# Softmax division moved from the exponents into the matmul that turns them, in two of three attention branches

## The chip, the cores and the metric

The kernel runs on one core of one Trainium2 chip. Its time is the device time of one execution in microseconds (us). Three runs of the kernel before gave 1705.82, 1708.54 and 1713.55 us; the median, 1708.54 us, is what a changed kernel is held against. Five engines work side by side, each through its own list of instructions in order, and wait for each other by semaphores: TensorE (PE, matmuls; PEld is its loading of the stationary operand), VectorE (DVE), ScalarE (ACT), GpSimd (POOL) and SyncE (SP, which issues most DMAs).

## The reference

One decoder layer on a sequence of 1024 positions, width 1024, in float32. Three attention branches read one combined projection of the normalised input:

- A: three head groups of four heads with strided windows, merged by their softmax denominators;
- B, the shared-key branch: eight query heads in two groups that share a key head each, window of 128, with a learned sink in each head's denominator;
- M, the memory branch: four heads of 128 against 256 memory tokens.

Then come gates, three output projections, one common output projection, and a feed-forward block. For B and M the part that matters here is

```python
lse = jax.nn.logsumexp(s, axis=-1)
if sink is not None:
    lse = jnp.logaddexp(lse, sink...)
p = jnp.exp(s - lse[..., None])
o = jnp.einsum('nhgbqk,nhbkd->nhgbqd', p, vw)      # B
p = jax.nn.softmax(sc, axis=-1)                    # M
o = jnp.einsum('bhsm,bmhd->bshd', p, mv)
```

In words: each row of exponents (one query, up to 256 keys) is divided by the row's sum, and the quotients weigh the values.

## The kernel before

The first part of the program, `input_projections`, handles 44 jobs (`JOBS`), each the projection of one tile of 128 positions for one branch. PE walks the jobs in order; a job of branch A or B has eight slices of 3 matmuls with 512 columns and eight of 3 matmuls with 256 columns (`project`), a job of M has only the 512-column ones. Everything else of the attention hangs between these slices at fixed places. The attention of a tile is cut into pairs (`PAIRS`): one pair per tile in A and M, two per tile in B, which makes 16 pairs in B and 8 in M. A pair holds four heads as two units `u` of two heads `e`. Pairs run two jobs behind their projection (`LAG`).

For pair n, four engines work in turn:

1. PE `score(n)` writes the four heads' scores to two PSUM banks (L1336 for B, L1332 for M).
2. DVE `minima(n)` finds each row's minimum of the negated scores and for B writes them, masked, to the tile `prob` (L1049; L1038 for M).
3. ACT `exps(n)` writes the exponents to `prob`, 128 queries in the partitions by up to 256 keys, and their sums to `small` (L832); for B it also takes the exponent of the sink (L838).
4. DVE `divide(n)`: for B it adds the sink (L1069), then takes the reciprocal of four sums (L1071) and multiplies the four heads' exponents in place (L1076). After each unit it raises `prob_done`.
5. PE `turn_probs(n, u)` turns the blocks of 128x128 of unit u by a transposition against `ident` into the PSUM bank `prob_turn` (L1350); that is four blocks, or two in the first tile of B, which has no tile before it. It raises `prob_turned`.
6. ACT `copy_probs(n, u)` copies them to SBUF (`prob_t`, L845).
7. PE `weigh_values(n)` multiplies by the values (L1373), and DVE `copy_out(n)` takes the result from PSUM (L1087).

The order in PE's list is written out by hand (`step_slices`, `second_turns`, `parts`). At the step of pair n stand `turn_probs(n - 1, 0)`, `score(n)`, `weigh_values(n - 2)` in a row; `turn_probs(n - 1, 1)`, called the second turn below, stands two slices later. In DVE's list `minima(n)`, `copy_out(n - 2)`, often `normalise` of the next tile's queries and keys (L998, L1005), and two or three slices on `divide(n)` (`DIVIDE_BEHIND`). Branch A isn't divided there; its sums are used later by `merge_factors`.

`rope_cos` and `rope_sin` are tables of 3 orders of the sequence; orders 1 and 2 serve the strided groups of A, order 0 serves A's first group and B. `prob` has room for two pairs.

Of the kernel before, what the change touches and what calls it, by code (L numbers as in the profile page):

```python
# [11 lines left out]
ALU = mybir.AluOpType  # L12
# [3 lines left out]
P = 128  # L16
# [20 lines left out]
KIND = [STAGES[s][0] for s, _ in JOBS]  # L37
# [88 lines left out]
def has_prev(j):  # L126

    s, t = JOBS[j]
    kind, order = STAGES[s][:2]
    if kind == "M":  # L130
        return True
    return t > 0 if order == 0 else (t % 2 == 1 if order == 1 else False)
# [215 lines left out]
def input_projections(nc, x_t, mem_t, positions, attn_norm, w_in, a_q_norm, a_k_norm, b_q_norm, b_k_norm,  # L348
# [8 lines left out]
    with ExitStack() as ctx:  # L357
# [14 lines left out]
        rope_cos = sb("rope_cos", [P, 3, 8, ROT])  # L372
        rope_sin = sb("rope_sin", [P, 3, 8, ROT])
# [6 lines left out]
        with ExitStack() as dilated:  # L380
# [13 lines left out]
        small = sb("small", [P, 2, 20])  # L394
# [26 lines left out]
        scored, min_done, exp_done, prob_done, prob_turned, prob_copied, pv_done, o_done, sink_gap, sink_exp = (  # L421
            sem(n) for n in ("scored", "min_done", "exp_done", "prob_done", "prob_turned", "prob_copied",
                             "pv_done", "o_done", "sink_gap", "sink_exp"))
# [21 lines left out]
        prob_turn = ps[:, PT, :].rearrange("p (e b n) -> p e b n", e=2, b=2)  # L445
# [93 lines left out]
        def prob_of(n, u):  # L539
            return prob[:, 2 * (n % 2) + u, :, :]  # L540

        def unit_stats(n, u, e):

            j, v = PAIRS[n]
            s, t = JOBS[j]
            i = 2 * u + e
            if KIND[j] == "A":
                return stats[:, STAGES[s][2], t, i:i + 1], stats[:, STAGES[s][2], t, 4 + i:5 + i]
            return small[:, n % 2, i:i + 1], small[:, n % 2, 4 + i:5 + i]
# [357 lines left out]
        def _(dve):  # L907
# [154 lines left out]
            def divide(n):  # L1062
                j, v = PAIRS[n]
                kind = KIND[j]
                dve.wait_ge(exp_done, 2 * n + 2)
                total = small[:, n % 2, 4:8]
                if kind == "B":
                    dve.wait_ge(sink_exp, count_b(n) + 1)
                    link(dve.tensor_tensor(small[:, n % 2, 12:16], total, small[:, n % 2, 8:12], ALU.add))  # L1069
                    total = small[:, n % 2, 12:16]  # L1070
                link(dve.reciprocal(small[:, n % 2, 16:20], total))  # L1071
                c0 = 0 if has_prev(j) else P
                for u in range(2):
                    for e in range(2):
                        i = 16 + 2 * u + e
                        ins = dve.tensor_scalar(prob_of(n, u)[:, e, c0:256], prob_of(n, u)[:, e, c0:256],  # L1076
                                                small[:, n % 2, i:i + 1], None, ALU.mult)
                        if e == 0:
                            link(ins)
                    ins.then_inc(prob_done, 1)  # L1080
# [77 lines left out]
            for j in range(NJ + LAG + 1):  # L1158
# [24 lines left out]
                for k in range(8):  # L1183
                    if k in step_slices(j):
                        n = steps_before(j) + step_slices(j).index(k)
# [31 lines left out]
        def _(pe):  # L1217
# [122 lines left out]
            def turn_probs(n, u):  # L1340
                j = PAIRS[n][0]
                if KIND[j] == "A":
                    pe.wait_ge(exp_done, 2 * n + u + 1)
                else:
                    pe.wait_ge(prob_done, 2 * count_bm(n) + u + 1)
                if n >= 1 or u:
                    pe.wait_ge(prob_copied, 2 * n + u)
                for e in range(2):
                    for b in range(0 if has_prev(j) else 1, 2):
                        ins = pe.transpose(prob_turn[:, e, b, :], prob_of(n, u)[:, e, b * P:(b + 1) * P], ident[:])  # L1350
                ins.then_inc(prob_turned, 1)

            def weigh_values(n):
# [1592 lines left out]
```

## Time and profile before

| what | value |
|---|---|
| median of three runs | 1708.54 us |
| the profiled execution | 1709.16 us |
| its span in the trace | 1707.4 us |
| PE busy | 1648.7 us (97%) |
| DVE busy | 927.6 us (54%) |
| ACT busy | 664.9 us (39%) |
| POOL busy | 968.6 us (57%) |

Durations below come from the one profiled execution; what lies outside its span is 1709.16 - 1707.4 = 1.8 us. The first turn of a pair of B after its division is at 366 us of the span, the last of M at 572.6 us; then the gates begin (580 us). "Idle before" in a row is the time in which the engine stood still ahead of that instruction, with what ended it. Matmuls overlap: the start of one and of the next show their true spacing, which is shorter than the duration of each.

### The profile page before, as it was taken

To read this page: it belongs to the slowest core of one execution; us is meant where nothing else is said; L and a number is where in the kernel's file an instruction comes from. 1 tells how busy PE (TensorE), PEld (TensorE's weight loads), DVE (VectorE), ACT (ScalarE), POOL (GpSimd) and SP (SyncE) were. 2 spreads that over 40 slices of the span, in tenths; PEclk is the share of its full clock that TensorE was granted. 3 is DMA by queue.
4 is the path that set the end of the run, shared out by engine and by line. 5 is a ranking of instruction groups with operands and counts; after the bars stand their busy time and mean duration, and the time that the engine had idled before them with its cause. 6 is when DMAs were issued, how large, how long until landed. Compare 5 with 4: busy or idle time off the path is not lost.

```text
span 1707.4 us, 22529 instructions
## 1 busy us (share of the span) xinstructions
PE 1648.7 (97%) x8518; PEld 1353.1 (79%) x8518; DVE 927.6 (54%) x1327; ACT 664.9 (39%) x1172; POOL 968.6 (57%) x729
## 2 busy tenths in 40 slices
PE   7999989989899989999999999999999999999999
PEld 5887878868778768888888887788888888788887
DVE  7455342457875672224554367888888888522001
ACT  5555565545544333335212325343343434322110
POOL 5643656542312477775245548999999997222221
PEclk9999999999999999999999999999999999999999
DMA  5113011111110323332655502222222322443311
GB/s 219 38 59 103 2 38 41 38 26 33 44 38 8 86 80 114 121 100 77 182 158 183 191 38 62 87 84 89 75 74 87 94 80 103 163 146 128 140 50 62
DMA packets 132904, 151.07 MB, mean 88 GB/s; under 512 B 15349, under 2 KB 95933, under 8 KB 132797
## 3 DMA queue, kind: packets, MB, share of 16 engines
q1 hardware_dynamic: 132364, 149.62, 27.4%
q8 instruction: 69, 1.13, 0.3%
q14 instruction: 39, 0.31, 0.1%
q10 hardware_dynamic: 432, 0.01, 0.0%
HBM read 116.98 MB, written 32.62 MB: 88 GB/s over the span
## 4 chain that ended last, share of the span: by engine, by line
PE 59%; POOL 3%; DVE 2%; DMA 1%; ACT 1%; issue 0%; SPq 0%; DVEq 0%; ACTq 0%; POOLq 0%
PE ps L2805 24%; PE ps L2890 13%; PE ps L2140 11%; PE ps L2180 6%; PE ps L2196 3%; PE ps L2131 1%; DMA w_raw<-in_w_out_dram 1%; POOL wo L1862 1%; POOL f_lo L2646 0%; PE ps L2189 0%; DVE ffn_area L2763 0%; POOL f_lo L1867 0%; DVE attn_lo L2755 0%; DVE t_all L2673 0%; POOL ffn_area L1880 0%
## 5 line engine op out<-in xcount | busy, mean ns | idle before, releaser
L2646 POOL TENSOR_TENSOR f_lo<-ffn_area,f_hi 128x1024 fp32r<-128x1024 f32 x85 | 200.8, 2382 | 20.3 <-ACT f_hi L2533 20.3
L2678 POOL TENSOR_TENSOR attn_lo<-ffn_area,attn_lo 128x512 fp32r<-128x512 f32 x44 | 58.5, 1330 | 194.4 <-ACT attn_lo L2595 194.3
L2805 PE MATMUL ps<-t_all,f_hi 128*128 128x512 f32 x528 | 164.1, 392 | 1.9 <-DVE t_all L2673 1.6
L2533 ACT ACTIVATE f_hi<-ffn_area 128x1024 fp32r<-128x1024 f32 x85 | 80.2, 946 | 188.8 <-PE ps L2805 178.4
L1867 POOL TENSOR_TENSOR f_lo<-ffn_area,f_hi 128x1024 fp32r<-128x1024 f32 (+1 forms) x42 | 99.9, 2381 | 73.6 <-ACT f_hi L1715 73.6
L2805 PE MATMUL ps<-act_hi,f_hi 128*128 128x512 f32 x336 | 133.3, 397 | 4.6 <-POOL f_lo L2646 4.6
L688 POOL TENSOR_SCALAR head_rstd<-head_ss 128x8 f32<-128x8 f32 (+2 forms) x42 | 11.0, 262 | 217.9 <-DVE head_ss L979 217.9
L2805 PE MATMUL ps<-act_hi,f_lo 128*128 128x512 f32 x336 | 132.3, 394 | 0.0
L2805 PE MATMUL ps<-act_lo,f_hi 128*128 128x512 f32 x336 | 131.2, 391 | 0.0
L1277 PE MATMUL ps<-w_hi,act_hi 128*128 128x512 f32 (+1 forms) x320 | 122.5, 383 | 5.3 <-DVE w_lo L504 2.6
L2805 PEld LDWEIGHTS ps<-t_all,f_hi 128*128 128x128 f32 x528 | 98.9, 188 | 24.5 <-DVE t_all L2673 1.6
L1277 PE MATMUL ps<-w_lo,act_hi 128*128 128x512 f32 (+1 forms) x320 | 112.3, 351 | 0.0
L1277 PE MATMUL ps<-w_hi,act_lo 128*128 128x512 f32 (+1 forms) x320 | 112.2, 351 | 0.0
L2805 PE MATMUL ps<-t_all,f_lo 128*128 128x512 f32 x264 | 103.4, 392 | 0.0
L845 ACT ACTIVATE prob_t<-ps 128x512 f32<-128x512 f32 (+1 forms) x96 | 50.4, 525 | 131.2 <-PE ps L1373 126.1
L2595 ACT ACTIVATE attn_lo<-ffn_area 128x512 fp32r<-128x512 f32 x44 | 27.8, 631 | 180.3 <-PE ps L2890 180.3
L699 POOL TENSOR_TENSOR qk<-qk,gains 128x256 f32<-128x256 f32 (+1 forms) x74 | 62.5, 845 | 50.2 <-DVE qk L1003 30.5
L2714 DVE TENSOR_TENSOR attn_out<-attn_out 128x1024 f32<-128x1024 f32 x22 | 72.0, 3274 | 24.8 <-ACT attn_out L2588 24.8
L2763 DVE TENSOR_TENSOR ffn_area<-ps,ffn_area 128x512 f32<-128x512 f32 x16 | 10.4, 692 | 131.9 <-PE ps L2890 131.6
L2196 PE MATMUL ps<-wo,act_hi 128*128 128x512 f32 x256 | 81.1, 398 | 0.2 <-POOL wo L1862 0.2
L2890 PE MATMUL ps<-act_hi,attn_lo 128*128 128x512 f32 x256 | 80.8, 395 | 0.0
L2805 PEld LDWEIGHTS ps<-act_hi,f_hi 128*128 128x128 f32 x336 | 63.5, 189 | 18.1 <-POOL f_lo L2646 5.0
(314 smaller groups left out, 4586.5 us busy)
## 6 DMA issues: line engine op xcount, KB each, us to landing
ffn_area<-in_w_up_dram SPq DMA_DIRECT2D x44, 512.0 KB, 5.2
gate<-gates SPq DMA_DIRECT2D x24, 512.0 KB, 3.7
ffn_area<-in_w_gate_dram SPq DMA_DIRECT2D x23, 512.0 KB, 5.2
z<-attn_out SPq DMA_DIRECT2D x22, 512.0 KB, 2.6
ffn_area<-in_w_down_dram SPq DMA_DIRECT2D x22, 512.0 KB, 4.1
ffn_area<-z SPq DMA_DIRECT2D x44, 256.0 KB, 2.9
gates<-ffn_area SPq DMA_DIRECT2D x40, 256.0 KB, 2.1
attn_out<-in_x_dram SPq DMA_DIRECT2D x16, 512.0 KB, 6.3
```

The costliest lines, as they stand in the source:

```text
L699: ins = pool.tensor_tensor(buf[:, h0:h1, :], buf[:, h0:h1, :], gains[:, off:off + dh].unsqueeze(1).to_broadcast([P, h1 - h0, dh]), ALU.mult)
L1277: ins = pe.matmul(dst, lhs, w[:, k, cols], start=(k == 0 and i == 0), stop=(k == 7 and i == 2))
L1867: pool.tensor_tensor(part_place(p, part, f_lo), part_source(p, part), part_place(p, part, f_hi).bitcast(F32), ALU.subtract).then_inc(w_lo_ ...
L2140: ins = pe.matmul(gate_bank(p, i), w[:, slot, cols], a[:, k, :], start=(k == 0 and m == 0), stop=(k == 3 and m == 2))
L2180: ins = pe.matmul(o_bank(at), w[:, i0 + i, :], a[:, t0 + i, HALF[half]], start=(i == 0 and m == 0), stop=(i == tiles - 1 and m == 2))
L2196: ins = pe.matmul(ps[:, n % 4, :], a[:, k, t * P:(t + 1) * P], wo[:, slot, w, :], start=(k == 0 and i == 0), stop=(k == NK - 1 and i == 2))
L2533: act.activation(part_place(p, part, f_hi, first_hi), part_source(p, part), ACT.Copy).then_inc(w_hi_done, 1)
L2646: pool.tensor_tensor(part_place(p, part, f_lo, first_lo), part_source(p, part), part_place(p, part, f_hi, first_hi).bitcast(F32), ALU.subt ...
L2678: pool.tensor_tensor(z_lo[:, m % 2, :], z_raw[:, m % 4, :], z_hi[:, m % 2, :].bitcast(F32), ALU.subtract).then_inc(z_lo_done, 1)
L2714: dve.tensor_tensor(conv[:, 0, :], conv[:, 0, :], conv[:, 1, :], ALU.mult).then_inc(z_done, 1)
L2805: ins = pe.matmul(out, w, a, start=(start and k == 0 and i == 0), stop=(stop and k == 3 and i == 2))
L2890: ins = pe.matmul(ps[:, BANK[i], :], z[a], w[b][:, HALF[half]], start=(k == 0 and n == 0), stop=(k == FT - 1 and n == 2))
```

## The change

`divide(n)` no longer touches `prob`. The four multiplications now have `ident` as their input and write four 128x128 diagonals with the reciprocals on them, of two heads each into the second and third orders of `rope_cos` (unit 0) and of `rope_sin` (unit 1), which nothing reads by then. `turn_probs` of branches B and M then is no transposition against `ident` but an ordinary float32 matmul of the same exponents with the diagonal as the moving operand: it turns and divides in one. Branch A keeps the transposition. Since there is one set of diagonals and not two, `divide(n)` first waits until both turns of pair n-1 are done (`prob_turned`).

```diff
+        def diagonal(u):
+            return (rope_cos, rope_sin)[u][:, 1:3].rearrange("p o t f -> p (o t f)").rearrange("p (e n) -> p e n", e=2)
@@ divide(n), DVE
                 link(dve.reciprocal(small[:, n % 2, 16:20], total))
-                c0 = 0 if has_prev(j) else P
+                if n >= 1:
+                    dve.wait_ge(prob_turned, 2 * n)
                 for u in range(2):
                     for e in range(2):
                         i = 16 + 2 * u + e
-                        ins = dve.tensor_scalar(prob_of(n, u)[:, e, c0:256], prob_of(n, u)[:, e, c0:256],
-                                                small[:, n % 2, i:i + 1], None, ALU.mult)
+                        ins = dve.tensor_scalar(diagonal(u)[:, e, :], ident[:], small[:, n % 2, i:i + 1], None, ALU.mult)
@@ turn_probs(n, u), PE
-                        ins = pe.transpose(prob_turn[:, e, b, :], prob_of(n, u)[:, e, b * P:(b + 1) * P], ident[:])
+                        dst, src = prob_turn[:, e, b, :], prob_of(n, u)[:, e, b * P:(b + 1) * P]
+                        if KIND[j] == "A":
+                            ins = pe.transpose(dst, src, ident[:])
+                        else:
+                            ins = pe.matmul(dst, src, diagonal(u)[:, e, :], start=True, stop=True)
```

No instruction changes its place. On PE, at a step of B (L1336 is a score, L1373 a weighing of values, L1277 a projection), the kernel before has, from the second turn of one pair to the score of the next:

```order
1713 L1350 MATMUL ps<-ident,prob 128x128 [waits prob_copied,prob_done]
1714 L1350 MATMUL ps<-ident,prob 128x128 x3
...
1721 L1277 MATMUL ps<-w_hi,act_hi 128x256 [waits normed,v_done]
1722 L1277 MATMUL ps<-w_lo,act_hi 128x256
1723 L1277 MATMUL ps<-w_hi,act_lo 128x256
1724 L1350 MATMUL ps<-ident,prob 128x128 [waits prob_copied,prob_done]
1725 L1350 MATMUL ps<-ident,prob 128x128 x3
1726 L1336 MATMUL ps<-k_ring,q_ring 128x128 [waits min_done,k_done,q_done]
```

The changed kernel at the same place (its lines are numbered 5 to 9 higher):

```order
1713 L1359 MATMUL ps<-rope_sin,prob 128x128 [waits prob_copied,prob_done]
1714 L1359 MATMUL ps<-rope_sin,prob 128x128 x3
...
1721 L1282 MATMUL ps<-w_hi,act_hi 128x256 [waits normed,v_done]
1722 L1282 MATMUL ps<-w_lo,act_hi 128x256
1723 L1282 MATMUL ps<-w_hi,act_lo 128x256
1724 L1359 MATMUL ps<-rope_cos,prob 128x128 [waits prob_copied,prob_done]
1725 L1359 MATMUL ps<-rope_cos,prob 128x128 x3
1726 L1341 MATMUL ps<-k_ring,q_ring 128x128 [waits min_done,k_done,q_done]
```

Rows and waits are the same; the moving operand of the turns is another, and the kind of matmul with it. On DVE, around one `divide` of B, the kernel before has (COPY k_ring and TENSOR_REDUCE serve the next tile, the ISA row is the next pair's `minima`):

```order
449 L1069 TENSOR_TENSOR small<-small 128x4 [waits sink_exp,exp_done]
450 L1071 RECIPROCAL small<-small 128x4 [waits dve_chain]
451 L1076 TENSOR_SCALAR prob<-prob,small 128x256 [waits dve_chain] x2
452 L1076 TENSOR_SCALAR prob<-prob,small 128x256
453 L1076 TENSOR_SCALAR prob<-prob,small 128x256 [waits dve_chain]
454 L1027 COPY k_ring<-ps 128x128 [waits pv_done,q_done,turned]
455 L979 TENSOR_REDUCE head_ss<-square 128x10 [waits rstd_done,sq_done]
456 L1049 ISA prob,small<-ps,masks,neg_sink 128x256 [waits prob_turned,scored]
```

and the changed kernel:

```order
452 L1074 TENSOR_TENSOR small<-small 128x4 [waits sink_exp,exp_done]
453 L1076 RECIPROCAL small<-small 128x4 [waits dve_chain]
454 L1082 TENSOR_SCALAR rope_cos<-ident,small 128x128 [waits prob_turned,dve_chain]
455 L1082 TENSOR_SCALAR rope_cos<-ident,small 128x128 [waits dve_chain]
456 L1082 TENSOR_SCALAR rope_sin<-ident,small 128x128
457 L1082 TENSOR_SCALAR rope_sin<-ident,small 128x128 [waits dve_chain]
458 L1032 COPY k_ring<-ps 128x128 [waits pv_done,q_done,turned]
459 L984 TENSOR_REDUCE head_ss<-square 128x10 [waits rstd_done,sq_done]
```

Four instructions of 256 columns became four of 128, and the first of them has a new wait, for PE's `prob_turned`.

## Rows read from the trace of the kernel before

**Rows 1.** The page, section 1: busy time, share, instructions.

```profile
PE 1648.7 (97%) x8518; PEld 1353.1 (79%) x8518; DVE 927.6 (54%) x1327; ACT 664.9 (39%) x1172; POOL 968.6 (57%) x729
```

**Rows 2.** Busy time by stretch: stretch, its us, each engine's busy us, granted clock, DMA.

```profile
500.00:580.00 80.00, 78.41 (x459) 65.47 (x457) 42.35 (x73) 32.40 (x87) 18.17 (x19) 1.00 0.14 35
360.00:500.00 140.00, 127.08 (x1006) 104.88 (x1005) 108.02 (x328) 71.20 (x224) 44.92 (x62) 0.98 0.14 38
```

**Rows 3.** Who waited for whom on PE, 360 to 580 us: total us, times, longest.

```profile
PE ps L1350 <- DVE prob L1076: 10.0, 11, 2.7
PE ps L1277 <- DVE qk L1005: 2.1, 2, 1.1
```

**Rows 4.** PE in order of time, branch M: start, us, instruction, count.

```profile
534.96 1.95 PE L1373 MATMUL ps<-prob_t,v_mem 128*128 128x128 f32 x16
536.67 0.48 PE L1277 MATMUL ps<-w_hi,act_hi 128*128 128x512 f32 x1
536.99 0.40 PE L1277 MATMUL ps<-w_lo,act_hi 128*128 128x512 f32 x1
537.22 0.39 PE L1277 MATMUL ps<-w_hi,act_lo 128*128 128x512 f32 x1
...
538.14 0.60 PE L1350 MATMUL ps<-ident,prob 128*128 128x128 f32 x4
538.49 0.48 PE L1277 MATMUL ps<-w_hi,act_hi 128*128 128x512 f32 x1
538.81 0.40 PE L1277 MATMUL ps<-w_lo,act_hi 128*128 128x512 f32 x1
```

**Rows 5.** PE's groups by line and shape, 500:580 (two rows) and 360:500 (last).

```profile
L1373 PE MATMUL ps<-prob_t,v_mem 128*128 128x128 f32 x128 | 15.7, 276 | 0.0
L1350 PE MATMUL ps<-ident,prob 128*128 128x128 f32 x64 | 9.9, 277 | 1.6 <-DVE prob L1076 0.8 <-PE ps L1277 0.3
L1350 PE MATMUL ps<-ident,prob 128*128 128x128 f32 x122 | 19.2, 276 | 9.2 <-DVE prob L1076 9.2
```

**Rows 6.** DVE in order of time: two divisions of four heads, by width.

```profile
370.59 1.13 DVE L1076 TENSOR_SCALAR prob<-prob,small 128x128 f32<-128x128 f32 x4
439.45 1.40 DVE L1076 TENSOR_SCALAR prob<-prob,small 128x256 f32<-128x256 f32 x4
```

**Rows 7.** All engines in order of time, around a division of B.

```profile
413.29 0.60 PE L1350 MATMUL ps<-ident,prob 128*128 128x128 f32 x4
415.19 1.88 DVE L1076 TENSOR_SCALAR prob<-prob,small 128x256 f32<-128x256 f32 x4
416.26 0.66 PE L1350 MATMUL ps<-ident,prob 128*128 128x128 f32 x4 [0.65 <-DVE prob L1076]
```

**Rows 8.** PE in order of time: rows with idle time before them.

```profile
366.00 0.44 PE L1350 MATMUL ps<-ident,prob 128*128 128x128 f32 x2 [0.75 <-DVE prob L1076]
380.07 0.35 PE L1277 MATMUL ps<-w_hi,act_hi 128*128 128x256 f32 x1 [1.12 <-DVE qk L1005]
382.61 0.66 PE L1350 MATMUL ps<-ident,prob 128*128 128x128 f32 x4 [1.96 <-DVE prob L1076]
468.39 0.66 PE L1350 MATMUL ps<-ident,prob 128*128 128x128 f32 x4 [2.67 <-DVE prob L1076]
```

**Rows 9.** PE and DVE in order of time, at another division of B.

```profile
389.04 0.60 PE L1350 MATMUL ps<-ident,prob 128*128 128x128 f32 x4
389.11 1.39 DVE L1076 TENSOR_SCALAR prob<-prob,small 128x256 f32<-128x256 f32 x4
392.05 0.60 PE L1350 MATMUL ps<-ident,prob 128*128 128x128 f32 x4
```

**Rows 10.** Busy time by stretch, two of 20 us in branch B.

```profile
380.00:400.00 20.00, 17.23 (x128) 14.40 (x128) 14.27 (x42) 8.58 (x27) 7.46 (x11) 0.91 0.34 93
460.00:480.00 20.00, 16.81 (x141) 13.24 (x141) 16.28 (x45) 8.84 (x26) 6.83 (x10) 0.91 0.14 41
```

**Rows 11.** Who waited for whom on PE, 580 us to the end: the longest.

```profile
PE ps L2131 <- POOL f_lo L1867: 6.7, 1, 6.7
```

## The prediction

> **What bounds the kernel now.** I read the page first: PE is busy 97% of the span [rows 1], so whatever is added to PE's list is likely to arrive in the time, and whatever is taken off another engine counts only where PE waits for it. Then I read the busy time by stretch. The change acts between about 360 and 580 us. In branch M (500:580) PE is busy 78.4 of 80 us: there it is the bound with nothing to spare. In branch B (360:500) it is busy 127.1 of 140 us and DVE 108.0 [rows 2]: 12.9 us are open. The waits say whose they are: eleven times PE stands before a turn for the division, 10.0 us in all, and twice before a projection for the normalised queries and keys, 2.1 us [rows 3]. The three waits for the division in M make only 0.8 of the 10.0 us [rows 5]. So the case is: DVE loses work for which PE waits 9.2 us in B, and PE gains work in all of B and M.
>
> **What a turn costs on PE, before and after.** The projections' matmuls start 0.23 us apart (536.99 to 537.22). Four transpositions begin at 538.14 and the second matmul behind them at 538.81; less the 0.23 of the matmul between them that is 0.44 us, or 0.11 us for one [rows 4]. The new operation, a float32 product of 128x128 exponents with 128 moving columns, isn't in the trace with a diagonal, but the same shape is: the weighing of values in M. There 8 pairs of 8 written products, 64 in all, leave 128 records [rows 5]: each float32 product is issued twice. Sixteen records begin at 534.96 and the second matmul behind them at 536.99; less 0.23 that is 1.80 us for 8 products, 0.225 us for one [rows 4]. The extra is 0.225 - 0.11 = 0.115 us a block. The bounds: by the bare distance to the next start the product costs 1.71 / 8 = 0.214 and the transposition 0.35 / 4 = 0.088 [rows 4]; the closest pairing is 0.214 - 0.11 = 0.104, the widest 0.225 - 0.088 = 0.137. I take 0.115, since it counts both blocks up to the same point behind them.
>
> The Trainium skill has a rule that prices this differently: the page "TensorE: Matmul & The Clock Gate", section "Terms", calls the transpose mode four times faster for FP32, and "FP8 and Floating Point Precision", section "TensorE Precision Notes", gives true FP32 four passes through the array. The trace has a factor of two between the two operations, 0.225 to 0.11, and the measurement decides; the factor of four is kept as a rival below.
>
> How many blocks: in B 16 pairs of 8, less 4 in each of the 2 pairs of the first tile, is 120; in M 8 pairs of 8 is 64 (64 records in 500:580, and 122 in 360:500, where the last of branch A stand too [rows 5]). Together 184. PE's list grows by 184 x 0.115 = 21.2 us (19.1 to 25.2 by the bounds): 13.8 in B, 7.4 in M.
>
> **What the waits take back.** A wait for the division shrinks in two ways. First, between the score of pair n and the first turn of pair n stands the second turn of pair n-1 (413.29, ahead of the waiting turn at 416.26 [rows 7]). Its 4 blocks grow by 0.46 us, and they fall into time in which PE would have stood. The first turn itself is behind the wait and ahead of the next score; its 0.46 us delay that score and everything that hangs on it, and nothing takes them back. Second, the division gets shorter: four writes of 128 columns last 1.13 us, four of 256 columns 1.40 us [rows 6], that is 0.07 us an instruction, and two of them stand before a first turn is released: 0.13 us. So each wait gives back at most 0.46 + 0.13 = 0.59 us.
> - Six of the eight waits of B are of full-size turns and longer than that, from 0.65 us [rows 7] to 2.67 us [rows 8]: 6 x 0.59 = 3.5.
> - The one at 366.00 has turns of two blocks [rows 8]: 0.23 + 0.13 = 0.36.
> - The wait for queries and keys at 380.07 and the one for the division at 382.61 follow each other, behind a second turn of two blocks [rows 8]: together 0.36. The other wait of the former kind, 2.1 - 1.12 = 0.9 us, takes 0.46 of its second turn.
> - The three of M are shorter than 0.59 each: all 0.8 us go.
>
> That is 3.5 + 0.4 + 0.4 + 0.5 + 0.8 = 5.5 us (5.48 unrounded).
>
> **What costs nothing, and what hides it.** The rest of DVE's saving, 0.07 us for each of 88 writes of full width or 6 us in all, lies where PE is at work on slices and not waiting; it counts only if DVE's queue is what is late next, which is bounded by the waits themselves (in the first rival). The new wait of `divide(n)` for both turns of pair n-1: behind it on DVE stand the key copy, the sums of squares and the next minima, and PE's first turn waits for it. At one place the second turn ends at 413.89, with its extra 0.46 at 414.35, and the division starts at 415.19 [rows 7]: covered by 0.8 us. At another it is not covered: the second turn ends at 389.64, now 390.10, and the division started at 389.11 [rows 9]. It comes 1.0 us later; its first unit is then done at about 390.10 + 0.6 = 390.7, and the turn that needs it stands at 392.05: the slices in between hide it, with 1.3 us to spare. ACT's copies come later by as much as the turns, and the weighing that needs them stands a whole step further. Behind 580 us PE's one long wait, 6.7 us for POOL [rows 11], begins with work that itself starts at 580; I take it, and all behind it, to move as one piece with the branches' end.
>
> **The sum.** 21.2 - 5.5 = +15.7 us. On the profiled execution, 1709.16 us, that gives 1724.9; on the median of the runs shown, which is 0.6 us lower, 1724.2. I predict 1724 us.
>
> **Rivals.**
> - *The idle time takes far more than I count.* If the lighter DVE removed all 12.1 us of waits [rows 3], and with them the two drops of the granted clock (0.91 in two stretches of 20 us, 2 x 20 x 0.09 = 3.6 us [rows 10]), the sum is 21.2 - 12.1 - 3.6 = +5.5: 1714 us, within what can't be told from no change. For it: DVE is busy 16.3 of 20 us where the longest wait is, and PE fell from 2.4 to 1.2 GHz only behind the two longest stands. Against it: the stands of 1.96 and 2.67 us shrink by 0.1 and 0.6 by my count and remain long, and the extra of the first turns, half of the whole, is ahead of the score from which each chain starts.
> - *Faster: the product costs PE no more than the transposition*, and DVE was the true bound of B. Then only the gains are left, at most the 12.1 us of waits and 3.6 us of clock: -15.7, 1693 us. It decides from an extra of about 0.02 us a block downward. For it: eight of the eleven waits are in B and all name the division. Against it: the 128 records for 64 products, and 0.13 us of shortening to a wait against 0.65 us and more of waiting.
> - *The new wait becomes the last one.* If it delayed the eight waiting divisions of B by the 1.0 us of the uncovered place, the sum is 15.7 + 8.0 = +23.7: 1732 us. For it: that place [rows 9]. Against it: it bites where the following turn doesn't wait, and the waiting ones have 0.8 us of cover [rows 7].
> - *A product at four times the transposition*, 0.44 us: 184 x 0.33 = 60.7, less 5.5, is +55: 1764 us. Against it: a product of that very shape at 0.225 us [rows 4].
> - That the change doesn't do what it says has no room here: the order of the instructions shows the operands replaced one for one.
>
> **How the numbers follow.** A measurement of this kernel can tell about 0.5%, 8.5 us, from no change: the border to slower is 1717. My forecast, 10 to 22 us more, has a chance of 0.74; the first rival, with what lies between it and the forecast, 0.13; the new wait 0.06; four times 0.03; faster 0.03; the rest, 0.01, near no change. The unknown costs reach from 19.1 - 12.1 - 3.6 = +3.4 to 25.2 - 5.5 = +19.7, with the new wait to +27.7. The range for 8 in 10 leaves the ends to the rivals: 1713 to 1731. Slower by over 0.5%: 0.74 + 0.06 + 0.03, and 0.01 of what lies between, 0.84. Within 0.5%: 0.12. Faster: 0.04.
>
> **What would show it.** In the changed kernel's profile: 2 x 184 = 368 records of the turns of B and M, in place of 184, and blocks of four that take about 0.9 us to the next matmul instead of 0.44; DVE's four writes at about 1.1 us; PE's waits for the division at about 5 us; 500:580 longer by 7 us, all of it PE's; the start of the gates 16 us later, and the same distance at the end. I am wrong if the turns leave one record each, if the waits in B vanish with the drops of the clock, if `prob_turned` is seen to release divisions for which PE then waits, or if the part behind the branches changes its own length.

## The result and the profile after

| | kernel before | changed kernel |
|---|---|---|
| median of 6 runs | 1709.14 us (1705.82 to 1713.55) | 1723.05 us (1720.47 to 1723.96) |
| ratio to before | 1 | 1.008, interval 1.0068 to 1.0092 |
| profiled execution | 1709.16 us, span 1707.4 | 1723.84 us, span 1722.0 |

The change makes the kernel 13.9 us slower; the forecast was 1724 us.

Section 1 of the page of the changed kernel, which answers to [rows 1]:

```profile
PE 1670.7 (97%) x8702; PEld 1377.9 (80%) x8702; DVE 921.7 (54%) x1327; ACT 666.0 (39%) x1172; POOL 968.6 (56%) x729
```

PE has 184 records more, 8702 against 8518: each of the 184 blocks leaves two where it left one. Its busy time rose by 22.0 us. DVE gave up 5.9 us, and PE stayed at 97%: the span grew with PE's work, by 14.6 of the 22.0 us.

To see where, I cut both traces at the same instructions of PE: the first turn of A's last pair, which is a transposition in both kernels and stands ahead of all turns of B, the first turn of B's last pair (right ahead of a memory score), and the first matmul of the gates. Busy time by stretch of the kernel before (columns as in [rows 2]), from the first cut to the second, and from the second to the third:

```profile
359.40:491.86 132.46, 119.54 (x956) 98.61 (x955) 103.19 (x318) 67.74 (x213) 42.62 (x59) 0.97 0.14 37
491.86:580.40 88.54, 86.62 (x512) 72.20 (x511) 47.52 (x85) 35.89 (x99) 20.66 (x22) 1.00 0.14 36
```

The same two stretches of the changed kernel, and the two of [rows 10]:

```profile
358.31:498.86 140.55, 132.58 (x1069) 113.43 (x1068) 99.20 (x320) 68.57 (x213) 43.34 (x59) 0.98 0.13 35
498.86:593.98 95.12, 94.07 (x583) 81.35 (x582) 45.07 (x82) 36.04 (x98) 20.70 (x22) 1.00 0.13 34
380.00:400.00 20.00, 18.11 (x140) 15.99 (x140) 12.31 (x40) 8.48 (x26) 6.34 (x9) 0.91 0.32 89
460.00:480.00 20.00, 17.23 (x133) 14.05 (x132) 15.74 (x45) 10.56 (x29) 5.69 (x8) 0.91 0.15 41
```

First stretch, 112 blocks: 8.1 us longer, with 13.0 us more work on PE and 5.0 us less idle time (12.92 to 7.97). Second stretch, 72 blocks (B's last 8 and M's 64): 6.6 us longer, with 7.45 us more work and 0.9 us less idle time (1.92 to 1.05). Together 14.7 us. Ahead of the first cut the changed kernel's execution happens to be 1.1 us earlier, behind the third it is 1.0 us later, and the spans differ by 14.6. Both stretches of 20 us still show a granted clock of 0.91: the drops did not go.

Who waited for whom on PE in the changed kernel, 355 to 600 us; it answers to [rows 3]:

```profile
PE ps L1359 <- DVE rope_cos L1082: 5.5, 5, 2.1
PE ps L1282 <- DVE qk L1010: 1.6, 2, 0.9
PE ps L1341 <- issue: 0.2, 1, 0.2
```

Eleven waits for the division became five, 10.0 us became 5.5, and none of them is left in M. The releaser is the write of the diagonals, `rope_cos` for unit 0. The turns themselves, PE in order of time in M; these rows answer to [rows 4]:

```profile
542.93 1.05 PE L1359 MATMUL ps<-rope_cos,prob 128*128 128x128 f32 x8
543.82 1.89 PE L1337 MATMUL ps<-k_mem,q_ring 128*128 128x256 f32 x8
...
548.72 1.05 PE L1359 MATMUL ps<-rope_sin,prob 128*128 128x128 f32 x8
549.53 0.48 PE L1282 MATMUL ps<-w_hi,act_hi 128*128 128x512 f32 x1
549.85 0.39 PE L1282 MATMUL ps<-w_lo,act_hi 128*128 128x512 f32 x1
```

Read as before, 549.85 - 548.72 - 0.23 = 0.90 us for four blocks, 0.225 each. A first turn is 0.89 us ahead of its score, where in M it was mostly 0.44.

The groups of turns in 500:580, records of both diagonals together 120, answer to the second of [rows 5]:

```profile
L1359 PE MATMUL ps<-rope_sin,prob 128*128 128x128 f32 x64 | 8.6, 277 | 0.3
L1359 PE MATMUL ps<-rope_cos,prob 128*128 128x128 f32 x56 | 7.4, 276 | 0.3 <-PE ps L1282 0.3
```

The two longest waits for the division, which answer to the last two of [rows 8]; they were 1.96 and 2.67 us:

```profile
381.92 1.66 PE L1359 MATMUL ps<-rope_cos,prob 128*128 128x128 f32 x8 [1.89 <-DVE rope_cos L1082]
473.74 1.34 PE L1359 MATMUL ps<-rope_cos,prob 128*128 128x128 f32 x8 [2.13 <-DVE rope_cos L1082]
```

The new wait, seen on DVE in the changed kernel at the place of [rows 9], with the two turns of PE around it:

```profile
388.87 1.05 PE L1359 MATMUL ps<-rope_sin,prob 128*128 128x128 f32 x8
...
390.03 0.61 DVE L1082 TENSOR_SCALAR rope_cos<-ident,small 128x128 f32<-128x128 f32 x2 [0.19 <-PE ps L1359]
390.56 0.61 DVE L1082 TENSOR_SCALAR rope_sin<-ident,small 128x128 f32<-128x128 f32 x2
...
392.32 1.05 PE L1359 MATMUL ps<-rope_cos,prob 128*128 128x128 f32 x8
```

DVE stands 0.19 us for the turn, writes the diagonals of unit 0 by 390.6, and PE, which has slices to do, takes them at 392.32 without a wait. Over both branches DVE stood for turns 0.7 us, three times.

### The profile page after: what moved, and what is told of

Its sections match the earlier page's. It is cut to its first block, busy times and chain, and to the rows that moved or that the text cites. A ratio compares the mean times of both kernels' runs of the same rounds, so it can differ in the third digit from the quotient of the medians.

```text
span 1722.0 us, 22921 instructions
## 1 busy us (share of the span) xinstructions
PE 1670.7 (97%) x8702; PEld 1377.9 (80%) x8702; DVE 921.7 (54%) x1327; ACT 666.0 (39%) x1172; POOL 968.6 (56%) x729
## 4 chain that ended last, share of the span: by engine, by line
PE 61%; POOL 2%; DVE 1%; ACT 0%; issue 0%; ACTq 0%; DVEq 0%; POOLq 0%
PE ps L2814 23%; PE ps L2899 13%; PE ps L2149 11%; PE ps L2189 7%; PE ps L2205 5%; PE ps L2140 1%; POOL f_lo L2655 0%; PE ps L2198 0%; DVE ffn_area L2772 0%; POOL f_lo L1876 0%; DVE attn_lo L2764 0%; POOL ffn_area L1889 0%; DVE t_all L2682 0%; POOL ffn_area L1886 0%; POOL ffn_area L1891 0%
```

## Experiments

All ratios are to the kernel before, which ran beside each kernel on the same chip; its medians were 1708.4 to 1709.6 us. A difference in us is the ratio less one, times that median. Three theories were open. The size of the product on PE decides, and the lighter division gives a little back (the forecast's). The rivals: DVE's lighter division is worth far more than counted and something else eats it; or the new wait costs something.

**The products alone.** The division as before; only the matmul of the turns of B and M is another, against the identity:

```diff
-                        ins = pe.transpose(prob_turn[:, e, b, :], prob_of(n, u)[:, e, b * P:(b + 1) * P], ident[:])
+                        dst, src = prob_turn[:, e, b, :], prob_of(n, u)[:, e, b * P:(b + 1) * P]
+                        if KIND[j] == "A":
+                            ins = pe.transpose(dst, src, ident[:])
+                        else:
+                            ins = pe.matmul(dst, src, ident[:], start=True, stop=True)
```

> The kernel before, but the turns of branches B and M are float32 products against the identity; the division on VectorE stays as it was. Theory (PE's second record a block is the whole loss, the waits take part of it back): 184 x 0.115 = +21.2 us of PE's list, less what the waits hide of the second turns (6 x 0.46, 0.23, 0.23, 0.46 and M's 0.8: 4.5), +16.7 us, ratio 1.0098; the waits for the division fall from 10.0 to about 6.5 us. Rival (VectorE's lighter division gave back much of the loss in the changed kernel): this kernel, which lacks that help, is slower than before by 19 to 25 us, ratio 1.011 to 1.015.

Measured: 1723.3 us, ratio 1.009 (1.0074 to 1.0105), +15.4 us. PE waited for the division 6.4 us in 8 places. So the products alone cost all of what the change costs; that they cost 1.5 us more lies within the two intervals.

**The diagonals alone.** The changed kernel with the transposition put back, so that DVE writes diagonals and waits for turns, but PE does its old work. This kernel leaves the division out of its result: the exponents of B and M stay undivided.

```diff
...
-                            ins = pe.matmul(dst, src, diagonal(u)[:, e, :], start=True, stop=True)
+                        ins = pe.transpose(prob_turn[:, e, b, :], prob_of(n, u)[:, e, b * P:(b + 1) * P], ident[:])
```

> The changed kernel, but the turns are transpositions against the identity again, so the exponents of B and M stay undivided; VectorE still writes the four diagonals and waits for the turns. It has VectorE's side of the change alone. Theory: eleven waits shorter by 0.13 us, -1.4 us, ratio 0.9992, between 0.997 and 1.001; the waits for the division 8 to 9 us. Rival (VectorE was the bound of branch B): -5 to -16 us, ratio 0.991 to 0.997. The new wait as a cost: a ratio above 1.001.

Measured: 1706.8 us, ratio 0.9991 (0.9982 to 1.0001), -1.5 us, with 8.5 us of waits for the division left in 10 places. The two parts add: 1.0090 and 0.9991 make 1.0081, and the whole change is 1.0080. The lighter division is worth about 1.5 us, by the interval between nothing and 3.1, in which the rival with 12 and more has no room.

**Each product twice.**

```diff
-                            ins = pe.matmul(dst, src, diagonal(u)[:, e, :], start=True, stop=True)
+                            for _ in range(2):
+                                ins = pe.matmul(dst, src, diagonal(u)[:, e, :], start=True, stop=True)
```

> The changed kernel with every product against a diagonal issued twice over (the same result): 184 products more. Theory: each is 0.225 us of PE, 41.4 us, of which the waits that are left (5.5 and 1.6 us) hide about 5: +36 us on the changed kernel, +50 us on the kernel before, ratio 1.029; waits for the division near 2 us. Rival (PE in branch B has far more room than its waits show, or the product is cheaper in a run of its own kind): under +35 us on the kernel before, ratio below 1.020. If the second turns, now 1.8 us long, make the division wait, more than +55.

Measured: 1758.6 us, ratio 1.0292 (1.0278 to 1.0306), +49.9 us. PE in order of time in M of this kernel:

```profile
543.54 1.95 PE L1360 MATMUL ps<-rope_cos,prob 128*128 128x128 f32 x16
545.33 1.89 PE L1337 MATMUL ps<-k_mem,q_ring 128*128 128x256 f32 x8
```

Eight products take 1.79 us, 0.224 each. The second set of 184 costs 1758.6 - 1723.05 = 35.5 us (36 by the ratios) where its own work is 184 x 0.225 = 41. Between the first cut and the third PE's idle time is 6.4 us here, 2.7 under the 9.0 of the changed kernel, and the second drop of the granted clock, worth up to 1.8 us, is missing here (1.00 in 440:500): together that is most of the difference. The waits for the division are still 4.1 us, in 3 places, where I had expected about 2.

**The new wait taken away** by a second set of diagonals in buffers that are free by then (odd pairs in `gains` and `masks`), so that a division waits only for the turns before the last pair's:

```diff
+            if n % 2:
+                return gains[:, 0:256].rearrange("p (e n) -> p e n", e=2) if u else masks[:, 1:4:2, :]
...
-                if n >= 1:
-                    dve.wait_ge(prob_turned, 2 * n)
+                if n >= 2:
+                    dve.wait_ge(prob_turned, 2 * n - 2)
```

> The changed kernel with two sets of diagonals (the second in tables that branches B and M don't use), so that a division waits for the turns of pair n-2, which are long done. Theory (the new wait costs nothing): the same as the changed kernel within 0.5 us, +13.9 us on the kernel before, ratio 1.008. Rival (the wait delays divisions for which PE then waits): up to 8 us faster than the changed kernel, ratio 1.0035 to 1.006.

Measured: 1723.5 us, ratio 1.008 (1.0067 to 1.0093), the same as the changed kernel; PE's waits for the division are 5.4 us in 5 places, as in the changed kernel. The new wait costs nothing that the runs can tell.

**Memory branch only.** Diagonals and products where `kind == "M"`, all else as in the kernel before (the edit is shown against the changed kernel):

```diff
-                if n >= 1:
+                if kind == "M":
                     dve.wait_ge(prob_turned, 2 * n)
...
+                        dst, src = (diagonal(u)[:, e, :], ident[:]) if kind == "M" else (prob_of(n, u)[:, e, c0:256],) * 2
...
-                        if KIND[j] == "A":
+                        if KIND[j] != "M":
```

> The change in the memory branch alone: diagonals, products and the new wait in M; the shared-key branch divides and transposes as before. Theory: 64 blocks by 0.115 us, 7.4 us, less M's waits of 0.8 us: +6.6 us, ratio 1.0039; the shared-key branch as before, its waits 9.2 us. Rival (the shared-key branch is the one that pays, since it holds two blocks in three): under +4.5 us, ratio below 1.0026.

Measured: 1715.5 us, ratio 1.0029 (1.0014 to 1.0045), +5.0 us: under the expectation of 6.6, within the interval's reach of it (2.4 to 7.7), and near the 5.7 that is left of the second stretch above without B's last 8 blocks. In this kernel's own trace the second stretch (490.15:584.43) is 94.28 us, 5.7 over the 88.54 before. The nine executions spread from 1709.0 to 1718.1 us, and the two medians lie 6.9 us apart, so the size isn't known more closely.

**First or second turns.** The products of the first experiment in only one turn of each pair. 92 blocks each, the same work on PE: 92 x 0.115 = 10.6 us.

```diff
-                        if KIND[j] == "A":          # against the first experiment
+                        if KIND[j] == "A" or u == 0:     # products in second turns; for first turns: or u == 1
```

Products in the second turns, ahead of the wait for the next division:

> The kernel before with float32 products against the identity in the second turns only (unit 1 of B and M); division as before. 92 blocks more by 0.115 us: 10.6 us on PE. Theory (a second turn stands ahead of the wait, so its growth falls into idle time): 4.5 us of it hidden, +6.1 us, ratio 1.0036. Rival (it doesn't matter where the growth stands): half of what both together cost (+15.4), +7.7 us, ratio 1.0045.

Products in the first turns, behind the wait:

> The kernel before with float32 products against the identity in the first turns only (unit 0 of B and M); division as before. 92 blocks more by 0.115 us. Theory (a first turn stands behind the wait and ahead of the next score, so nothing hides it): +10.6 us, ratio 1.0062, the waits for the division stay at 10 us. Rival (where it stands doesn't matter): +7.7 us, ratio 1.0045.

Measured: second turns 1713.4 us, ratio 1.0028 (1.0017 to 1.0040), +4.8; first turns 1720.1 us, ratio 1.0065 (1.0051 to 1.0078), +11.1. The same work costs less than half in the one place. Who waited for whom on PE, with the products in the second turns:

```profile
PE ps L1352 <- DVE prob L1076: 6.0, 9, 1.9
```

And with them in the first turns:

```profile
PE ps L1354 <- DVE prob L1076: 9.7, 9, 2.8
```

The growth ahead of the wait is paid out of the wait (10.0 us before, 6.0 now); behind the wait nothing is (9.7). PE's idle time between the first cut and the third says the same: 14.8 us before, 10.3 with the products in the second turns, 14.0 with them in the first. The profiled execution of the latter is the slowest of its six (1724.4 us) and has the clock at 0.83 and 0.88 in the stretches of [rows 10], so only its waits are read here. Together the two ratios give 1.0093, and both at once, the first experiment, 1.0090.

**No division at all.** The exponents of B and M stay undivided: only the sums' reciprocals are formed, and their end releases both turns.

```diff
-                link(dve.reciprocal(small[:, n % 2, 16:20], total))
...
-                        ins = dve.tensor_scalar(prob_of(n, u)[:, e, c0:256], prob_of(n, u)[:, e, c0:256],
-                                                small[:, n % 2, i:i + 1], None, ALU.mult)
+                dve.reciprocal(small[:, n % 2, 16:20], total).then_inc(prob_done, 2)
```

> The kernel before without the four multiplications of a division (the reciprocal stays and releases the turns): exponents of B and M stay undivided. It shows how much the division on VectorE can be worth at most. Theory: a first turn waits for two multiplications of 0.35 us less, 0.7 us: six waits by 0.65 to 0.7, the first by 0.5, the one at 382 by 0.7, M's 0.8 go: -6 to -7 us, ratio 0.996. Rival (the waits and the clock's drops all hang on VectorE's load): -12 to -16 us, ratio 0.991 to 0.993, waits for the division near 0 and no stretch with a granted clock of 0.91.

Measured: 1698.0 us, ratio 0.9937 (0.9924 to 0.9951), -10.8 us. Neither my 6 to 7 nor clearly the rival's 12 to 16. Who waited for whom on PE in this kernel, 355 to 600 us:

```profile
PE ps L1268 <- DVE qk L1005: 2.1, 2, 1.1
PE ps L1341 <- DVE small L1071: 2.4, 3, 1.0
PE ps L1341 <- ACT prob_t L845: 1.7, 2, 1.5
```

The waits fell by 7.6 us, from 10.0 to 2.4, with 1.7 new ones for ACT. I had counted 0.7 us for the two writes ahead of each first turn, from writes that stand alone; beside POOL two of them take up to 1.76 us, as the next experiment's rows show. From the first cut to the third this kernel takes 211.2 us, 9.8 less than before: PE's idle time is 6.8 us less and its busy time 3.0 less. Part of the busy time is the granted clock: of the two drops of [rows 10] the one at 380 us is still there (0.98 in 360:380 and 0.93 in 380:400), the one in 460:480 is gone (1.00), worth up to 20 x 0.09 = 1.8 us. But the clock as a whole gives nothing back in this execution: in the 40 us from the start of the gates it is 0.87 (569:609) where it was 0.91 at the same work (580:620), 1.6 us, and in the 60 us around PE's later stand for POOL 0.94 (1030:1090) where it was 0.97 (1040:1100), 1.8 us. How the 4 us above my count split isn't settled. So most of the wait is DVE's, here taken off by leaving out the writes altogether. The change keeps all 96 of them and only halves the columns of 88.

**The division unit by unit.** Sum, reciprocal and writes of unit 0 no longer wait for unit 1's exponents; the sink's exponent is taken after unit 0's. PE's work is as before.

```diff
                 for u in range(2):
+                    dve.wait_ge(exp_done, 2 * n + u + 1)
+                    total = small[:, n % 2, 4 + 2 * u:6 + 2 * u]
...
+                    link(dve.reciprocal(small[:, n % 2, 16 + 2 * u:18 + 2 * u], total))
```

> The kernel before, with the division done unit by unit: VectorE starts on the first two heads when their exponents are there, and ScalarE takes the exponent of the sink between the two units. It is meant to beat both kernels. Theory (where PE waits 0.65 to 1.06 us for a division, VectorE stands idle for ScalarE's last exponents, so the first unit can be ready 1 us earlier): the waits for the division fall from 10.0 to about 5 us, -5 us, ratio 0.997; the two longest, where VectorE's own queue is late, stay. Rival (the four added small instructions a pair, which take 0.4 us and more on VectorE, eat it up): within 2 us of the kernel before.

Measured: 1706.3 us, ratio 0.9984 (0.9974 to 0.9994), -2.7 us; waits for the division 6.1 us in 6 places. A gain, half of what I expected. DVE and POOL in order of time in this kernel, around one division of B:

```profile
413.70 0.29 DVE L1005 TENSOR_TENSOR qk<-ps,head_rstd 128x128 f32<-128x128 f32 x1
...
414.07 1.84 POOL L699 TENSOR_TENSOR qk<-qk,gains 128x512 f32<-128x512 f32 x2 [2.58 <-DVE qk L1005]
...
414.30 1.76 DVE L1077 TENSOR_SCALAR prob<-prob,small 128x256 f32<-128x256 f32 x2
...
416.36 0.74 DVE L1077 TENSOR_SCALAR prob<-prob,small 128x256 f32<-128x256 f32 x2
```

The same two writes take 1.76 us while POOL multiplies the queries by the gains, and 0.74 us when it has finished. POOL's product is released by DVE's own last multiplication of the normalised keys (L1005), right ahead of the division. So the division walks into the work that DVE has itself just released, and it is unit 0, for which PE waits, that pays. That happens once a tile, at every other division: up to 433 us five pairs of writes of unit 0 start just behind POOL and take 1.70 to 1.76 us, the four others take 0.61 to 0.74, and unit 1's never take more than 0.74.

**The keys' product behind the division.** If that is so, releasing POOL later should help. First with the whole division ahead of it, all else as before:

```diff
+                if kind == "B" and j + 1 - LAG >= 0 and KIND[j + 1 - LAG] == "B":
+                    later.append(second)         # the product that raises normed
...
                             at(divide, steps_before(j) + step_slices(j).index(step))
+                            while later:
+                                later.pop()()
```

> The kernel before with only the second product of B's normalised keys put behind the whole division; the division stays in one piece. Theory (GpSimd's product holds the division up): the eight waits of B shrink from 9.2 us by 0.4 us each and more where the division was held longest, to 4 to 6 us, but PE may now wait up to 0.3 us for the keys at each of seven tiles: ratio 0.996 to 0.999. Rival (the division's length is its own): ratio 1.000 or above, the waits moved from the turns to the projections.

Measured: 1714.0 us, ratio 1.0031 (1.0019 to 1.0043), +5.3 us, where I expected a gain. Who waited for whom on PE, 355 to 600 us:

```profile
PE ps L1286 <- DVE qk L1007: 11.2, 6, 3.7
PE ps L1359 <- DVE prob L1083: 4.2, 6, 1.5
```

DVE and PE in order of time at the longest:

```profile
447.73 1.39 DVE L1083 TENSOR_SCALAR prob<-prob,small 128x256 f32<-128x256 f32 x4
449.04 0.28 DVE L1007 TENSOR_TENSOR qk<-ps,head_rstd 128x128 f32<-128x128 f32 x1
...
449.47 0.36 PE L1286 MATMUL ps<-w_hi,act_hi 128*128 128x256 f32 x1 [3.73 <-DVE qk L1007]
```

The four writes take 1.39 us there, without POOL beside them, and the waits for the division fell from 10.0 to 4.2 us. But the same product frees the bank into which PE writes the next keys, and PE now stands 11.2 us for it, where it stood 2.1. The wait moved and grew.

**Unit by unit, and the keys' product between the units.** The two edits together, the product behind unit 0's writes:

> The kernel before with the division unit by unit, and with the small second product of B's normalised keys (it is what releases GpSimd's product with the gains) put behind the first unit's division. In the kernel with the division unit by unit alone, two multiplications that began 0.23 us behind that GpSimd product took 1.76 us in place of 0.7. Theory (VectorE's multiplications in SBUF are held while GpSimd's product runs): the first unit is divided ahead of it, the waits for the division fall from 6.1 to 3 us or less, ratio 0.994 to 0.997, the best of all kernels. Rival (the late normalised keys now hold up PE and GpSimd, or the waits hang on ScalarE): no faster than with the units alone, ratio 0.998 to 1.001.

Measured: 1704.1 us (8 runs, 1702.2 to 1706.4), ratio 0.9975 (0.9964 to 0.9985), -4.3 us: the lowest median of all that keep the division, though its interval overlaps that of the division unit by unit, and a little short of the 0.994 to 0.997 that I had expected. Waits for the division 3.1 us in 4 places, for the keys 4.3 us in 3. DVE and POOL in order of time:

```profile
410.58 0.74 DVE L1084 TENSOR_SCALAR prob<-prob,small 128x256 f32<-128x256 f32 x2
...
411.61 1.82 POOL L699 TENSOR_TENSOR qk<-qk,gains 128x512 f32<-128x512 f32 x2 [3.63 <-DVE qk L1007]
...
411.83 1.75 DVE L1084 TENSOR_SCALAR prob<-prob,small 128x256 f32<-128x256 f32 x2
```

Here unit 0's writes take 0.74 us and unit 1's, for which nobody waits yet, take 1.75. And, in this kernel, the two stretches in which the clock was 0.91 before, with one more:

```profile
380.00:400.00 20.00, 18.80 (x166) 15.82 (x167) 16.35 (x53) 8.55 (x28) 8.82 (x14) 1.00 0.37 94
460.00:480.00 20.00, 16.43 (x127) 12.05 (x125) 18.34 (x55) 10.70 (x35) 5.99 (x9) 1.00 0.11 27
340.00:360.00 20.00, 18.06 (x113) 15.37 (x111) 6.71 (x25) 7.73 (x27) 8.95 (x15) 0.91 0.00 1
```

The clock stayed at its upper level, 2.4 GHz, through both. This isn't a gain of the whole execution: a drop stands in 340:360 (the last row), where the kernel before has 1.00, and behind the branches the clock is as low as in the kernel without a division (0.87 in 573:613, 0.94 in 1034:1094). What the order itself gave is seen in PE's idle time from the first cut to the third, 11.5 us against 14.8.

## Why the prediction was right

- **PE's growth.** Predicted 13.8 us in B and 7.4 in M, by 0.225 - 0.11 a block. By busy time B's 112 blocks cost 13.0 us (0.116 each; predicted 12.9), and the 72 blocks behind cost 7.45 where the prediction has 8.3. The starts of PE's instructions in the two traces, each counted from its cut, show it more closely: a group of four blocks puts what stands behind it 0.45 us later (0.40 where PE waited for it before), 7.9 us for the 72, 0.110 a block. So the term of M was mis-sized by 0.4 us. The other 0.5 us lies in how idle time is read: a matmul of 512 columns is shown busy for 0.39 us though the next can start after 0.23, so 0.16 us of each wait behind one count as busy, and M's three waits are 0.4 to 0.5 us each and not the 0.24 to 0.30 that their rows show.
- **What the waits give back.** Predicted 5.5 us, 4.7 in B and 0.8 in M (the terms as written add up to 5.52, not 5.48). The idle time fell by 5.0 in the first stretch and 0.9 in the second, 5.8 in all. By the starts it is 6.1 us, and term by term: at each of the six full-size waits of B 0.52 to 0.57, together 3.2 (predicted 3.5); at the wait of [rows 7], for example, the turn starts 3.12 us later than before, counted from the first cut (418.29 and 416.26), where the projection behind the second turn starts 3.64 later (416.19 and 413.64). The waits at 380.07 and 382.61 gave 0.5 (0.36), the other one for the keys 0.35 (0.46), M's three 1.3 (0.8). And 0.6 us came from idle time ahead of a score ("issue", 0.84 to 0.20), which no step had. The term of 0.36 us for the wait at 366.00 was wrong altogether, it gave nothing:

```profile
364.90 0.71 PE L1359 MATMUL ps<-rope_cos,prob 128*128 128x128 f32 x4 [0.74 <-DVE rope_cos L1082]
```

  It was 0.75 us. The second turn ahead of it is of branch A and stays a transposition, and the division that it waits for had 128 columns before, too. So that the total came out near 5.5 is partly luck: one term that wasn't there, against about 1.1 us that weren't counted. The mechanism holds: that it is the second turns that are paid out of the waits, and not the first, is shown by the two halves, +4.8 against +11.1 us.
- **DVE's shortening.** Counted at 0.13 us a wait, about 1 us over eight. Of the 0.52 to 0.57 us at the six waits the second turn's growth is 0.45 to 0.46, which leaves 0.06 to 0.11. The diagonals alone measured -1.5 us, with an interval from -3.1 to 0.2: the size is confirmed, not more closely.
- **The new wait.** Predicted at nothing: 1.008 with it and without it, and 5.5 against 5.4 us of waits. That rival fell.
- **The idle time as the big prize.** The rival took all the waits for DVE's. No division at all gives -10.8 us, so most is indeed DVE's; but diagonals in place of divided exponents reach 1.5 of it. The stands of 1.96 and 2.67 us stayed 1.89 and 2.13, and both drops of the clock are still there in the changed kernel's execution; the last section shows that the second drop doesn't hang on the stand alone.
- **A product at four times the transposition.** Fell by the trace, 0.225 us to 0.11, and by the doubled product, 0.224.
- **Behind the branches.** The gates began 13.6 us later (16 foreseen), and the end was 14.6 later. Of the 1.0 us behind, 0.8 arise after PE's one long stand, which is 6.7 us as in [rows 11]: PE starts again 13.6 us later (609.30, now 622.88), and the first product of L2140 (now L2149) with `t_all` behind it is 14.4 us later (627.5, now 641.9). The fall of the clock itself is as long in both. Before:

```profile
604.00:608.00 4.00, 0.00 (x0) 0.00 (x0) 4.00 (x2) 0.30 (x1) 4.00 (x2) 0.74 0.00 0
608.00:612.00 4.00, 2.70 (x6) 2.17 (x7) 4.00 (x2) 0.00 (x0) 4.00 (x2) 0.50 0.33 67
612.00:616.00 4.00, 4.00 (x17) 3.28 (x16) 4.00 (x2) 0.00 (x0) 4.00 (x2) 0.90 0.56 195
```

The changed kernel:

```profile
620.00:624.00 4.00, 1.12 (x3) 0.93 (x4) 4.00 (x2) 0.00 (x0) 4.00 (x2) 0.67 0.01 2
624.00:628.00 4.00, 4.00 (x11) 3.13 (x10) 4.00 (x2) 0.00 (x0) 4.00 (x2) 0.50 0.79 251
628.00:632.00 4.00, 4.00 (x18) 3.23 (x18) 4.00 (x2) 0.00 (x0) 2.52 (x1) 0.98 0.04 13
```

  Counted as time at the upper level it is 4 x (0.26 + 0.50 + 0.10) = 3.4 us before and 4 x (0.33 + 0.50 + 0.02) = 3.4 after, but more of it lies where PE works again. PE has another stand for POOL, of 4.55 us, in both (it ends at 1070.61 and at 1084.68), and there the fall is longer in the changed kernel's execution: 0.77, 0.50 and 0.88 in the three stretches of 4 us from 1080, 3.4 us, against 0.77 and 0.80 in the two from 1068, 1.7 us; 0.6 us arise behind it, and 0.3 are made up in between. It isn't the change's own, as far as the runs tell: with two sets of diagonals, the same code behind the gates took 1718.7 - 591.6 = 1127.1 us, as the kernel before (1707.4 - 580.4 = 1127.0), where the changed kernel's execution took 1722.0 - 594.0 = 1128.0. "Moves as one piece" held to 1.0 us, and about as much differed ahead of the branches without any cause in the change.

My own misses lie in the experiments. In two (no division at all, unit by unit) I took DVE's writes at their undisturbed length; in the deferred product I watched one wait of PE and not what else the moved instruction releases.

## What to carry to other kernels

Before moving work onto the engine that is busy 97%, price it per instruction from a product of the same type and shape in the trace: two records a block were there to be read before the change. Then ask for each added piece whether it stands ahead of a wait of its engine (it is paid out of the wait) or behind it (it is paid in full), since the same 10.6 us cost 4.8 or 11.1 us. To shorten a wait for another engine, look at what that engine has just released: here two edits of the order, with the division's small instructions split by unit and no arithmetic changed, gave 4.3 us.

## What the runs showed of the hardware

- DVE's products from and to SBUF stand while POOL multiplies in SBUF: two writes of 128x256 take 0.74 us alone and 1.75 to 1.76 beside POOL's two products of 128x512, and two writes of 128x128 from the identity take 0.61 us alone and 1.55 beside them. POOL, DVE and PE of the changed kernel at such a place:

```profile
398.73 1.83 POOL L704 TENSOR_TENSOR qk<-qk,gains 128x512 f32<-128x512 f32 x2 [3.76 <-DVE qk L1010]
...
399.10 1.55 DVE L1082 TENSOR_SCALAR rope_cos<-ident,small 128x128 f32<-128x128 f32 x2
...
400.57 0.74 DVE L1082 TENSOR_SCALAR rope_sin<-ident,small 128x128 f32<-128x128 f32 x2
...
400.70 1.16 PE L1359 MATMUL ps<-rope_cos,prob 128*128 128x128 f32 x8 [0.25 <-DVE rope_cos L1082]
```

  DVE's pair ends when POOL's does, at about 400.6. The kernel before at the same place:

```profile
398.01 1.81 POOL L699 TENSOR_TENSOR qk<-qk,gains 128x512 f32<-128x512 f32 x2 [3.31 <-DVE qk L1005]
...
400.03 0.66 PE L1350 MATMUL ps<-ident,prob 128*128 128x128 f32 x4 [0.77 <-DVE prob L1076]
```

  There the turn starts 2.02 us behind POOL's product, now 1.97: beside POOL the length of a write is not its own, and half the columns gave 0.05 us. That is one reason why the halving gave so little; the other is in [rows 6], 0.07 us a write where DVE is alone. The Trainium skill says in "SBUF — State Buffer", section "Who interferes with whom", that VectorE (DVE) in a 2-port perf mode, which `tensor_scalar` can enter, and GpSimd contend for a shared pair of ports: whoever issues first holds it for the whole instruction, and "the other fully blocks (not throttle)". The trace agrees as far as it goes: POOL starts first at these places, and DVE's two writes end with POOL's product, 1.76 us against 0.74. Which mode DVE ran in no run shows.
- A float32 product of 128x128 with 128 columns takes PE 0.225 us and a transposition of the same tile 0.11: a factor of two, over 184 blocks and again with the product doubled.
- The two drops of the granted clock in B don't follow from the length of PE's longest stand alone. With 1.89 and 2.13 us both stretches are at 0.91 in the changed kernel. With two sets of diagonals the stands are 1.89 and 2.06 us, and only the first stretch is at 0.91:

```profile
460.00:480.00 20.00, 17.31 (x139) 13.68 (x138) 16.74 (x48) 12.09 (x35) 5.68 (x8) 1.00 0.15 45
```

  In the kernel with both edits of the order the longest stand is 2.2 us, and both stretches are at 1.00, but 340:360 is at 0.91 behind a stand of 1.94 us, where the kernel before stood 1.89 us and kept 1.00. What settles it is left open; each drop is worth at most 1.8 us.
